# Retention's values as 512-column products in four PSUM banks, gated linear attention's states as 64x64 products

## What is computed

```python
(rq, rk, rv, rg, gq, gk, gv, glr, gg, fq, fk, fv, ff) = jnp.split(h @ w_in, split_points, axis=-1)
...
ret = retention(heads(rq, RET_DK), heads(rk, RET_DK), heads(rv, RET_DV))
ret = head_group_norm(ret, ...)        # subtracts each head's mean
...
def gla(q, k, v, log_a):               # chunks of 64 rows, 4 heads, dk = 64, dv = 128
    ...
    kv = jnp.einsum('bnjhd,bnjhe->nbhde', kc * jnp.exp(b_end - b_cum), vc)
    def step(st, inp):
        a_n, kv_n = inp
        st = a_n[..., None] * st + kv_n
        return st, st
    _, s_all = lax.scan(step, jnp.zeros((b, h, dk, dv), F32), (a, kv))
    o = jnp.einsum('bnihd,nbhde->bnihe', qc, s_all)
```

## Time and profile before

| what | value |
|---|---|
| median of three executions | 2996.48 us (2991.75 to 2998.78) |
| the profiled execution's own time | 2995.28 us |
| its span, first to last instruction | 2993.5 us |
| PE busy | 2936.0 us, 98% of the span |
| PE's granted clock, mean over the span | 0.994 of full speed |
| ACT, DVE, POOL busy | 36%, 36%, 39% |
| mean busy share of the 16 DMA engines | 36% |

### The profile page before, as it was taken

One profiled execution on the slowest core, in us unless ns is written; L12 is line 12 of the kernel. 1 busy time (PEld: TensorE's weight loads), 2 busy tenths in 40 slices (PEclk: granted clock), 3 DMA queues, 4 the chain that ended last, 5 costly groups with the idle time before them and its releaser, 6 DMA issues.

```text
span 2993.5 us, 36662 instructions
## 1 busy us (share of the span) xinstructions
PE 2936.0 (98%) x15563; PEld 2449.8 (82%) x15563; DVE 1071.3 (36%) x1862; ACT 1090.1 (36%) x1657; POOL 1176.5 (39%) x502
## 2 busy tenths in 40 slices
PE   7999999999999999999999999999999999999999
PEld 4877878898888888788898888988888877888887
DVE  2544365256664633232142220342110266521102
ACT  3424433343332433442244332333222266432221
POOL 1432235334445433234434444434444333344442
PEclk9999999999999999999999999999999999999999
DMA  6332244335555422233333333333333322233332
GB/s 214 99 99 64 75 152 154 92 115 188 193 186 177 113 76 59 61 85 95 98 90 101 98 91 97 96 92 98 93 97 97 88 82 67 72 98 94 96 97 73
DMA packets 523799, 315.09 MB, mean 105 GB/s; under 512 B 15954, under 2 KB 496884, under 8 KB 523380
## 3 DMA queue, kind: packets, MB, share of 16 engines
q1 hardware_dynamic: 523636, 312.75, 35.5%
HBM read 310.61 MB, written 2.10 MB: 104 GB/s over the span
## 4 chain that ended last, share of the span: by engine, by line
PE 93%; DVE 3%; DMA 2%; ACT 1%; issue 0%; SPq 0%; DVEq 0%; ACTq 0%
PE b L427 21%; PE b L429 21%; PE b L428 21%; PE o L427 5%; PE o L428 5%; PE o L429 5%; DMA raw<-in_w_in_dram 2%; PE b L468 1%; PE b L469 1%; PE b L470 1%; PE b L586 1%; PE o L779 1%; PE s L662 1%; PE b L957 1%; PE b L958 0%; PE b L959 0%
## 5 line engine op out<-in xcount | busy, mean ns | idle before, releaser
L2596 POOL TENSOR_TENSOR lo<-raw,hi 128x1024 fp32r<-128x1024 f32 (+1 forms) x492 | 1174.4, 2395 | 1778.7 <-ACT hi L1220 1778.0
L427 PE MATMUL b<-HH,hi 128*128 128x512 f32 x1792 | 713.8, 398 | 3.3 <-DVE rq L2008 3.0
L429 PE MATMUL b<-HH,lo 128*128 128x512 f32 x1792 | 699.0, 390 | 0.0
L428 PE MATMUL b<-HL,hi 128*128 128x512 f32 x1792 | 698.6, 390 | 0.0
L1220 ACT ACTIVATE hi<-raw 128x1024 fp32r<-128x1024 f32 (+1 forms) x492 | 508.9, 1039 | 462.1 <-DMA raw<-in_w_down_dram 105.8
L427 PEld LDWEIGHTS b<-HH,hi 128*128 128x128 f32 x1792 | 336.8, 188 | 83.1 <-issue 12.1
L428 PEld LDWEIGHTS b<-HL,hi 128*128 128x128 f32 x1792 | 337.0, 188 | 71.1 <-issue 2.2
L429 PEld LDWEIGHTS b<-HH,lo 128*128 128x128 f32 x1792 | 336.6, 188 | 71.2
L427 PE MATMUL b<-FH,hi 128*128 128x512 f32 (+1 forms) x594 | 218.0, 367 | 0.0
L428 PE MATMUL b<-FL,hi 128*128 128x512 f32 (+1 forms) x594 | 217.1, 365 | 0.0
L429 PE MATMUL b<-FH,lo 128*128 128x512 f32 (+1 forms) x594 | 217.1, 365 | 0.0
(11 more groups left out here) (464 smaller groups left out, 4494.2 us busy)
## 6 DMA issues: line engine op xcount, KB each, us to landing
raw<-in_w_ada_dram SPq DMA_DIRECT2D x96, 512.0 KB, 5.0
raw<-in_w_up_dram SPq DMA_DIRECT2D x88, 512.0 KB, 4.0
raw<-in_w_in_dram SPq DMA_DIRECT2D x80, 512.0 KB, 4.2
raw<-in_w_mg_dram SPq DMA_DIRECT2D x48, 512.0 KB, 3.8
raw<-in_ffn_w_gate_dram SPq DMA_DIRECT2D x44, 512.0 KB, 3.8
raw<-in_ffn_w_up_dram SPq DMA_DIRECT2D x44, 512.0 KB, 3.8
raw<-in_w_down_dram SPq DMA_DIRECT2D x32, 512.0 KB, 4.0
raw<-in_ffn_w_down_dram SPq DMA_DIRECT2D x32, 512.0 KB, 3.9
```

What stands on the lines that cost most here:

```text
L427: e.matmul(out, wh, xh, start=start and k == 0, stop=False)
L428: e.matmul(out, wh, xl, start=False, stop=False)
L429: mm = e.matmul(out, wl, xh, start=False, stop=stop and k == last)
L2596: e.tensor_tensor(t["lo"][:, s, 0:w], K.raw[:, s, 0:w], t["hi"][:, s, 0:w].bitcast(F32), ALU.subtract).then_inc(*m.lo.up(n))
```

## The change

Retention's values are made in one call. For each of four chunks j, which now hold 256 rows x 512 columns of the weights, all four blocks of 128 rows get six matmuls of 512 columns, and the sums stay in four banks (b0, b1, `o`, b2) until the last chunk. The banks are named by hand and no longer taken from the rotation, and `turn` is set to 0 when the stage of retention's attention begins. ACT and DVE read one bank per row block, with as many instructions as before. In gated linear attention each matmul of the states becomes two, one per head, with 64 stationary columns and 128 moving ones, written to the half of the partitions in which the result is read.

```diff
@@ schedule
         drain(P.ret_inputs(l))
-        for c in range(2):
-            drain(P.ret_values(l, c))
+        drain(P.ret_values(l))
...
-        P.order = ["b0", "b1"]
+        P.order, P.turn = ["b0", "b1"], 0
@@ TensorSteps
-    def ret_values(self, l, c):
-        m = self.m
-        yield from self.project_rows(self.w, 1024 + 256 * c, [("rv", l, c, u) for u in range(2)],
-                                     lambda u: m.atake.at("rv", l, c, u))
+    def ret_values(self, l):
...
+        e, q, m, t, free = self.e, self.q, self.m, self.t, self.free
+        banks = ("b0", "b1", "o", "b2")
+        for j in range(4):
+            n = self.weight(self.w, 256 * j, 2, 1024, 512)
+            hi, lo = self.K.slot(n, 2, 512)
+            q.wait_ge(m.lo.at(n))
+            for r, b in enumerate(banks):
+                out, c = self.bank[b], slice(r * 128, r * 128 + 128)
+                q.wait_ge(free[b] if j == 0 else None)
+                for kk in range(2):
+                    k = 2 * j + kk
+                    H_, L_ = t["HH"][:, k, c], t["HL"][:, k, c]
+                    e.matmul(out[:, :], H_, hi[:, kk, :], start=(k == 0), stop=False)
+                    e.matmul(out[:, :], H_, lo[:, kk, :], start=False, stop=False)
+                    mm = e.matmul(out[:, :], L_, hi[:, kk, :], start=False, stop=(k == 7))
+                done = ([("rv", l, r)] if j == 3 else []) + ([("chunk", n)] if r == 3 else [])
+                if done:
+                    mm.then_inc(*m.dense.up(*done))
+            yield None
+        for r, b in enumerate(banks):
+            self.K.where["rv", l, r] = b
+            free[b] = m.atake.at("rv", l, r)
@@ TensorSteps.gla_attention
             for n in range(8):
-                c0, r = 64 * (n % 2), n // 2
-                mm = e.matmul(bank[kvb[n % 2 + n // 4 * 2]][:, (n // 2 % 2) * 256:(n // 2 % 2) * 256 + 256],
-                              t["ED"][c0:c0 + 64, r // 2, (r % 2) * 256 + p2 * 128:(r % 2) * 256 + p2 * 128 + 128],
-                              t["gv"][c0:c0 + 64, r, p2 * 256:p2 * 256 + 256], start=True, stop=True)
+                rows, r = slice(64 * (n % 2), 64 * (n % 2) + 64), n // 2
+                for hh in range(2):
+                    c1 = (r % 2) * 256 + 128 * hh
+                    k1 = (r % 2) * 256 + p2 * 128 + 64 * hh
+                    mm = e.matmul(bank[kvb[n % 2 + n // 4 * 2]][64 * hh:64 * hh + 64, c1:c1 + 128],
+                                  t["ED"][rows, r // 2, k1:k1 + 64],
+                                  t["gv"][rows, r, p2 * 256 + 128 * hh:p2 * 256 + 128 * hh + 128], start=True, stop=True)
```

More of the change, by code:

```diff
@@ L669, in value @@
             ob = ("o", "t0")[h % 2]
-            q.wait_ge(m.vattn.at("rp", l, n), *[m.atake.at("rv", l, c, u) for c in range(2) for u in range(2)],
+            q.wait_ge(m.vattn.at("rp", l, n), *[m.atake.at("rv", l, r) for r in range(4)],
                       free[ob] if j == 0 else None)
@@ L1358, in ret_inputs, with ret_values @@
             jobs[i], 64, 1.0, t["rT"][:, i % 2, :], m.vtake.at(*jobs[i - 2]) if i >= 2 else None))
-    def ret_values(self, l, c):
+    def ret_values(self, l):
         e, q, m, t = self.e, self.q, self.m, self.t
[L1363 to L1373, removed]
+        for j in range(4):
+            self.chunk()
+            yield None
+        for r in range(4):
+            out = self.bank[self.K.where.get(("rv", l, r), "b0")]
+            q.wait_ge(m.vtake.at("rvm", l, r))
+            for h in range(4):
+                c = slice(128 * h, 128 * h + 128)
+                a = e.activation(t["rv"][:, r, c], out[:, c], ACT.Identity, bias=t["RVM"][:, 4 * r + h:4 * r + h + 1])
+            a.then_inc(*m.atake.up(("rv", l, r)))
     def ret_attention(self, l):
@@ L2027, in ret_inputs, with ret_values @@
         yield from self.projects(jobs, 2 * l, take)
-    def ret_values(self, l, c):
+    def ret_values(self, l):
         e, q, m, t = self.e, self.q, self.m, self.t
[L2032 to L2041, removed]
+        for j in range(4):
+            self.next_chunk()
+            yield None
+        for r in range(4):
+            N = t["RVM"][:, 4 * r:4 * r + 4]
+            q.wait_ge(m.dense.at("rv", l, r), m.atake.at("rv", l - 1, r) if l else None)
+            e.tensor_reduce(N, self.out_of(("rv", l, r))[:, :].rearrange("p (n c) -> p n c", c=128), AXX,
+                            ALU.add).then_inc(*m.vtake.up(("rvs", l, r)))
+            q.wait_ge(m.vtake.at("rvs", l, r))
+            e.tensor_scalar(N, N, -1.0 / 128, None, ALU.mult).then_inc(*m.vtake.up(("rvm", l, r)))
     def ret_attention(self, l):
```

## The result

The changed kernel takes 2999.89 us (median of 16 executions, 2996.51 to 3004.69), the kernel before, timed beside it, 2995.44 us (16 executions, 2991.75 to 2998.78). The ratio is 1.0016, 95% interval 1.0009 to 1.0023: **4.45 us slower**. About 5.3 us are to be explained.

A forecast was written before the change was run, and what follows sets the result against it. PE was taken to bound the kernel, busy 2936.0 of 2993.5 us. Terms -2.55 + 4.65 + 0.72 - 3.68 = -0.86 us moved the median from 2996.48 to 2995.6 us; range 2991.5 to 3002.0.

The forecast's parts named there:

- part 2: Values' first matmul in each layer waits for b0 until DVE has read rk's last tile: +4.65 us in all.
- part 3: Shifted rotation: at two norms, three matmuls come behind PE's wait for DVE, 0.36 us each norm, +0.72 us.
- a rival, at 13%: The clock falls at the new b0 waits: 2997.3 us with one fall, 2999.0 us with two; 13%.
- one row, the wait of 1.49 us: Argument against clock falls: at PE's wait at 83.09, amid dense matmuls, the clock stayed at 1.00.
- Part 1: Values as 96 matmuls of 512 columns per layer instead of 192 of 256: 21.76 us per layer, together -2.55 us.
- the value product behind them: First value product after the values' matmuls: slack of 5.2 us covers the last bank's read, so no cost.
- Part 4: States as 32 smaller pieces per group, priced by L505's row: 0.92 us saved per group, -3.68 us for four.
- floor of about 62 ns: Skill's floor under each matmul: states' 32 pieces take 1.98 us, nothing saved; the related rival gave 2999.3 us, 15%.
- the slower rival: States' quarters don't run side by side: +1.93 us per group, +7.7 for four, 3007.0 us; 5%.
- I cost that at nothing: Values' weight chunks: slots come back one by one, second and fourth up to 1.7 us later; costed at nothing.
- the signs named: Expected in the profile: named waits, stretches and group times, and granted clock 1.00 behind the two new waits.
- wrong if: Prediction wrong if a wait over a microsecond appears at an unnamed place, above all first value product or weight chunk.

The follow-up runs named there:

- e3: The changed kernel with rotation and norm waits as before; the values still begin in the bank of rk's last tile: 2998.23 us, before 2995.87.
- e4: The changed kernel with rotation and norm waits as before, the values beginning in banks long free: 2991.34 us, before 2995.87.
- e1: The kernel before with only the new loop of the states: 2993.55 us, before 2995.87.
- e2: The changed kernel with the old loop of the states, so only the values' half of the change: 3004.12 us, before 2995.87.
- e5: The changed kernel with the rotation as before; the values' second row block meets the bank of rk's last tile: 2994.59 us, before 2996.42.
- e7: e4 with 48 unread single-column matmuls added at the start of PE's stream: ratio 0.9981 to the kernel before.
- e8: The changed kernel with `o` joining the dense rotation from each layer's start and the values beginning in a bank long free: 2983.60 us, before 2996.42.
- e6: The kernel before with only the rotation's turn set to 0 where retention's attention begins: 2996.16 us, before 2996.42.

## Why the prediction was wrong

**The step that failed is part 2's "Cost: +4.65"**, with part 3's "+0.72" beside it: both price a wait at its length. Each lengthened wait can also bring a fall of the clock, which costs PE 1.7 us of the matmuls behind it. This was a rival, at 13% and for the two waits of part 2 only, at 2997.3 or 2999.0 us. The argument against it was one row, the wait of 1.49 us in the midst of dense matmuls where the clock stayed at 1.00. That row is right, and no profile here shows a fall at a wait of 1.5 us in such a stretch. But the new waits are 2.2 us, nearer to the 2.7 of L779, where a fall was on the table: I took the nearer surroundings over the nearer length.

A nearer row still was overlooked. The stretch from 212 to 216, with the clock at 0.57, stands in the prediction without its cause, and it lies behind a wait of nearly the length of the new ones, in the kernel before:

```profile
211.88 0.38 PE L517 MATMUL t<-retR,CON 32*128 32x128 f32 x2 [2.26 <-DVE retR L2060]
```

From 212 to 216 PE was busy without a pause, from 213.6 on with dense matmuls. The same profile has waits of 2.45 and 2.60 us at L779 behind which the clock stayed up:

```profile
290.00:296.00 6.00, 4.50 (x23) 1.00 0.01 3
1189.00:1195.00 6.00, 5.26 (x25) 1.00 0.00 0
```

So of its five waits of 2.2 to 2.8 us on PE behind the start-up three had a fall (2.26, 2.62 and 2.75 us) and two had none. That gives a fall at each new wait a chance of about a half, where the rival had 13% for either. The rival also left out that part 3 moves two waits from 1.8 and 1.5 to 2.1 and 1.8 us, where the clock had held in the profiles of before and now sometimes doesn't. Over all executions of the changed kernel the clock costs 5.1 ±0.8 us more than before, three falls' worth; e3 against e4 puts 2.2 ±0.9 of it on the waits for b0, and the changed kernel against e3 1.8 on the norms. The rest is within the errors.

**Part 1 was right.** Without a fall the values take 21.76 us: in e4 from 110.44 to 132.20. That the value product behind them would not wait was right too.

**Part 2's length was right**: the first matmul starts 111.33 - 108.77 = 2.56 us after the last of `rk`, where it was 0.22 in the earlier trace rows, 2.34 more; in layer 1 1046.16 - 1043.61 = 2.55, also 2.3 more.

**Part 3's length was right**, 0.36 in the one (1.77 to 2.13) and 0.35 in the other (1.47 to 1.82).

**Part 4 was right**, 0.89 us per group and 3.6 in all, and e1 alone saves 3.1 ±0.5. The floor of about 62 ns that the Trainium skill gives for matmuls decoded in microcode (TensorE: Matmul & The Clock Gate, Back-to-back issue gap) isn't there: these pieces come every 32 ns. Quarters that split rows and columns at once run side by side, so the slower rival is out as well.

**The sum at full clock**: -0.86 forecast, -1.0 ±0.5 measured. That they agree is in part luck, since a second step was wrong: "I cost that at nothing", said of the chunks, with the reason that "that cover would have to go before a late transfer reached PE". Late transfers did reach PE, and the `foxT` waits grew by 3.0 us, though not by the mechanism that I had weighed: the changed number of instructions moved PE's fetches onto two chunks. What they cost stays open. In e2 to e5, the remainder is 1.4 to 2.8 us above the computed sum; in e7, with one late landing fewer, 0.2 above; in the changed kernel itself nothing. The single times of these kernels scatter too much to settle it.

Of the signs named, the granted clock failed: it was to be 1.00 behind both new waits and was 0.66 over the 5 us behind each. No wait of more than a microsecond appeared at a new place, so the "wrong if" was not met to the letter, but two waits for weight chunks, already over 2 us, grew by 1.3 and 1.5.

## What to carry to other kernels

Where one engine is busy for 98% of the span, count a new wait on it at its length and then ask of the clock. List the engine's waits with the granted clock behind each, find the *shortest* ones behind which it fell, and give every new wait of that length or more a fall as a chance, by how many of its like had one. One wait of the same length at which the clock held proves nothing: here waits of 2.45 and 2.60 us without a fall stand beside one of 2.26 with it. A fixed choice of bank next to a rotation is a change of the rotation too: follow the last tenant of each bank at every place behind it, since a bank that nobody uses at that point (`o` here) can take away more waits (e8: 12.8 us) than the arithmetic saves. Where two kernels differ by a thousandth, split the spans of all executions by their granted clock before believing what one profile shows.

## What the hardware showed that I had not expected

- A single wait of 2.2 us between dense matmuls brought PE from 1.00 to 0.50 of its clock for about 3.5 us of uninterrupted work, 1.7 us lost; the fall came after the wait had ended. At 2.2 us it came in five of the six waits for `rk` that the profiles of the changed kernel, e2 and e3 hold; at the norms' waits it came in five of the six of 1.8 and 2.1 us that the profiles of the changed kernel, e2 and e6 hold, but by the means of all executions in perhaps half. Where the wait at the norm ahead of layer 1 is that of before (1.8 us) one profile of seven has a fall, e7's. At the waits of 1.5 us for `rq` and `X` there is none in any profile. Over all of PE's waits that the timelines of the twelve profiles list from 70 us on, and of at least 0.9 us: up to 1.58 us a fall at none of 78, from 1.66 to 1.93 at 10 of 28, from 2.13 to 3.10 at 35 of 50, from 3.46 on at all 15. So there is no sharp edge in the length: the same wait of 1.9 us in the second block, which no edit touches, has a fall in four profiles of twelve.
- Sixteen matmuls of one column at the start of the program, 3000 us long, made one weight chunk at 288 us take 7.02 us from issue to landing instead of 5.17 and lengthened PE's wait there from 2.45 to 4.29 us. A 16 KB fetch of instructions (122 of them move 2.00 MB) fell within its transfer.
